# Expert products with a straight read and a PSUM write in four rounds

## The reference

```python
def chunk(args):
    hc, ec, gc = args                       # tokens, chosen experts, their gates
    u = peer_u[ec]
    a = jax.nn.gelu(jnp.einsum("ckd,cd->ck", u, hc).astype(jnp.float32)) * gc
    vv = peer_v[ec]
    return jnp.einsum("ck,ckd->cd", a.astype(vv.dtype), vv)
```

## Time and profile before

| | |
|---|---|
| median of 3 runs | 1580.08 us (1580.06 to 1580.09) |
| the profiled execution, its own time | 1579.2 us |
| its span in the trace | 1577.1 us |
| TensorE clock granted, mean | 0.999 |
| instructions | 33476 |
| scores, about | 325 to 697.6 us |
| values, about | 697.6 to 1062.9 us |

### The profile page before, as it was taken

How to read it: one execution, slowest core, us unless ns; L and a number is a source line. 1 busy time by engine, 2 the same in 40 slices (tenths; PEclk the granted TensorE clock), 3 DMA queues, 4 the chain that set the end, 5 groups by cost and what they waited for, 6 DMA issues and landing times.

```text
span 1577.1 us, 33476 instructions
## 1 busy us (share of the span) xinstructions
PE 1563.8 (99%) x12568; PEld 1472.5 (93%) x12568; DVE 1069.8 (68%) x1867; ACT 881.2 (56%) x1251; POOL 883.7 (56%) x413
## 2 busy tenths in 40 slices
PE   9999999999999999999999999999999999999998
PEld 8999899999999999998888888889999999999998
DVE  7998743879933777778888666676937484455522
ACT  6567766454454444444444445557677654676653
POOL 8786468978886000000000244458875689888886
PEclk9999999999999999999999999999999999999999
DMA  6564335555555555555555655566543356665563
GB/s 222 173 197 154 107 122 192 194 178 195 188 187 189 171 177 171 178 166 175 179 178 163 219 190 190 195 195 188 178 140 111 118 165 190 195 197 190 188 196 124
DMA packets 86217, 277.03 MB, mean 176 GB/s; under 512 B 11232, under 2 KB 18160, under 8 KB 86128
## 3 DMA queue, kind: packets, MB, share of 16 engines
q1 hardware_dynamic: 85712, 274.76, 54.0%
q0 software_dynamic: 272, 1.05, 0.2%
q10 hardware_dynamic: 144, 0.00, 0.0%
HBM read 274.73 MB, written 1.05 MB: 175 GB/s over the span
## 4 chain that ended last, share of the span: by engine, by line
PE 92%; issue 2%; DVE 2%; POOL 2%; ACT 2%; DMA 0%; SPq 0%; DVEq 0%; ACTq 0%; POOLq 0%
PE gemm L683 35%; PE gemm L986 22%; PE gemm L688 18%; PE aux L1272 4%; PE gemm L817 3%; PE aux L966 2%; POOL w_lo L466 1%; PE gemm L704 1%; PE gemm L729 1%; ACT w_hi L1368 1%; PE gemm L1272 1%; PE aux L936 0%; PE gemm L803 0%; PE gemm L710 0%; PE gemm L746 0%
## 5 line engine op out<-in xcount | busy, mean ns | idle before, releaser
L466 POOL TENSOR_TENSOR w_lo<-raw,w_hi 128x1024 fp32r<-128x1024 f32 (+1 forms) x330 | 789.4, 2401 | 282.9 <-ACT w_hi L1368 279.1
L1368 ACT ACTIVATE w_hi<-raw 128x1024 fp32r<-128x1024 f32 (+1 forms) x492 | 514.9, 1048 | 560.5 <-PE gemm L683 310.2
L683 PE MATMUL gemm<-h_hi,w_hi 128*128 128x256 f32 x2096 | 289.2, 280 | 1.1 <-ACT w_hi L1368 1.0
L683 PE MATMUL gemm<-h_lo,w_hi 128*128 128x256 f32 x2144 | 289.9, 277 | 0.0
L688 PE MATMUL gemm<-h_hi,w_lo 128*128 128x256 f32 x2096 | 284.6, 278 | 2.4 <-POOL w_lo L466 1.5
L683 PEld LDWEIGHTS gemm<-h_lo,w_hi 128*128 128x128 f32 x2144 | 266.0, 188 | 0.3 <-issue 0.2
L683 PEld LDWEIGHTS gemm<-h_hi,w_hi 128*128 128x128 f32 x2096 | 261.3, 188 | 4.2 <-issue 1.6
L466 DVE TENSOR_TENSOR w_lo<-raw,w_hi 128x1024 fp32r<-128x1024 f32 x162 | 195.7, 1223 | 102.0 <-ACT w_hi L1368 101.7
L688 PEld LDWEIGHTS gemm<-h_hi,w_lo 128*128 128x128 f32 x2096 | 259.8, 188 | 4.8 <-POOL w_lo L466 3.4
L986 PE MATMUL gemm<-w_hi,act_parts 128*128 128x512 f32 x1008 | 251.0, 391 | 0.4 <-ACT act_parts L1569 0.4
L986 PEld LDWEIGHTS gemm<-w_hi,act_parts 128*128 128x128 f32 x1008 | 188.2, 188 | 38.8 <-issue 0.5
(11 more groups left out here) (436 smaller groups left out, 2044.4 us busy)
## 6 DMA issues: line engine op xcount, KB each, us to landing
raw<-in_w_u SPq DMA_DIRECT2D x128, 512.0 KB, 3.5
raw<-in_w_ev SPq DMA_DIRECT2D x128, 512.0 KB, 3.6
raw<-in_w_up SPq DMA_DIRECT2D x48, 512.0 KB, 3.6
raw<-in_w_gate SPq DMA_DIRECT2D x24, 512.0 KB, 3.7
raw<-in_w_down SPq DMA_DIRECT2D x24, 512.0 KB, 3.5
raw<-in_w_conv_in SPq DMA_DIRECT2D x16, 512.0 KB, 4.4
raw<-in_w_peer_q SPq DMA_DIRECT2D x16, 512.0 KB, 4.0
raw<-in_w_branch SPq DMA_DIRECT2D x24, 288.0 KB, 2.8
```

The source lines that it names most:

```text
L466: eng.tensor_tensor(w_lo[v][:, 0:n], raw[c.raw][v][:, 0:n], w_hi[v][:, 0:n], ALU.subtract).then_inc(lo_ready[v], 1)
L683: mm = pe.matmul(spread(out), w[:, k, :], spread(act_part[:, k, :]), start=(n == k == 0), stop=False)
L1368: act.activation(w_hi[v][:, 0:n], raw[c.raw][v][:, 0:n], ACT.Copy).then_inc(hi_ready[v], 1)
```

## The change

In both expert stages the moving operand is read straight, while PSUM is written in four rounds. A column thus lands in another place of the bank: the columns read as g*64 + j*4 + c (256 of them) are written to j*16 + g*4 + c. `by_groups` names the straight order in the same four indices; gelu, which becomes two activations a chunk, one for each tile's 256 columns, and the four final copies read PSUM in four rounds and write straight, so everything behind them finds the columns as before. All other products keep `spread` on both sides.

```diff
+        def by_groups(tile):
+            return tile.rearrange("p (g j c) -> p g j c", g=4, c=4)
+        def whole(tile):
+            return tile
...
-                        mm = pe.matmul(spread(out), w[:, k, :], spread(act_part[:, k, :]), start=(n == k == 0), stop=False)
+                        mm = pe.matmul(psum_order(out), w[:, k, :], moving_order(act_part[:, k, :]), start=(n == k == 0), stop=False)
...
-                    mm = pe.matmul(spread(out), w[:, k, :], spread(x[0][:, k, :]), start=False, stop=(k == steps - 1))
+                    mm = pe.matmul(psum_order(out), w[:, k, :], moving_order(x[0][:, k, :]), start=False, stop=(k == steps - 1))
...
-                        product(c, P, it)
+                        product(c, P, it, moving_order=whole, psum_order=spread)
...
-                                mm = pe.matmul(gemm[2 * half + tt][:, :], a[:, c.raw, v, tt * P:(tt + 1) * P],
-                                               w[v][:, half * (D // 2):(half + 1) * (D // 2)],
+                                mm = pe.matmul(spread(gemm[2 * half + tt][:, :]), a[:, c.raw, v, tt * P:(tt + 1) * P],
+                                               whole(w[v][:, half * (D // 2):(half + 1) * (D // 2)]),
...
-                act.activation(act_peer[:, plane, :], pair(gemm[c.bank]),
-                               ACT.Gelu_apprx_tanh).then_inc(evacuated[c.bank], 1)
+                for v in range(2):
+                    ins = act.activation(by_groups(plane[v]), spread(pair(gemm[c.bank])[:, v, :]),
+                                         ACT.Gelu_apprx_tanh)
+                ins.then_inc(evacuated[c.bank], 1)
...
-                act.activation(experts[:, 1, half * (D // 2):(half + 1) * (D // 2)], gemm[2 * half + 1][:, :],
+                act.activation(by_groups(experts[:, 1, half * (D // 2):(half + 1) * (D // 2)]),
+                               spread(gemm[2 * half + 1][:, :]),
...
-                dve.tensor_copy(experts[:, 0, half * (D // 2):(half + 1) * (D // 2)],
-                                gemm[2 * half][:, :]).then_inc(experts_moved[0], 1)
+                dve.tensor_copy(by_groups(experts[:, 0, half * (D // 2):(half + 1) * (D // 2)]),
+                                spread(gemm[2 * half][:, :])).then_inc(experts_moved[0], 1)
```

More of the change, by code:

```diff
@@ L657, in _, with product @@
         def _(pe):
-            def product(c, m, it=None, x=(h_hi, h_lo), steps=KD):
+            def product(c, m, it=None, x=(h_hi, h_lo), steps=KD, moving_order=spread, psum_order=spread):
                 for v in range(2):
-                    product_tile(c, v, m, it, x, steps)
+                    product_tile(c, v, m, it, x, steps, moving_order=moving_order, psum_order=psum_order)
             def bank_free(c, it=None):
@@ L667, in bank_free, with product_tile @@
                     pe.wait_ge(evacuated[c.bank], c.bank_use - 1)
-            def product_tile(c, v, m, it=None, x=(h_hi, h_lo), steps=KD, rest=None, between=None):
+            def product_tile(c, v, m, it=None, x=(h_hi, h_lo), steps=KD, rest=None, between=None,
+                             moving_order=spread, psum_order=spread):
                 if v == 0:
@@ L974, in _ @@
                         gate_planes(0, s + 1, it)
-                    product(plan["u"][HALF + s], P, it)
+                    product(plan["u"][HALF + s], P, it, moving_order=whole, psum_order=spread)
             def expert_values(c, it, opens=False):
@@ L1013, in one @@
                     def one(w, a, half, tt, ends=False):
-                        return pe.matmul(gemm[2 * half + tt][:, :], a[:, c.raw, v, tt * P:(tt + 1) * P],
-                                         w[v][:, half * (D // 2):(half + 1) * (D // 2)], start=False, stop=ends,
+                        return pe.matmul(spread(gemm[2 * half + tt][:, :]), a[:, c.raw, v, tt * P:(tt + 1) * P],
+                                         whole(w[v][:, half * (D // 2):(half + 1) * (D // 2)]), start=False, stop=ends,
                                          skip_group_check=True)
@@ L1563, in gelus @@
                         round_weights(order[c.index + 1], it)
-                        gelu(c, bass.ds(it * 2 * BANKS + 2 * s, 2), it)
+                        gelu(c, [act_peer[:, bass.ds(it * 2 * BANKS + 2 * s + v, 1), :].rearrange("p o t -> p (o t)") for v in range(2)], it)
             def round_acts(c, plane, it=0):
```

## The result

The changed kernel takes 1586.09 us (median of 6 runs, 1585.48 to 1588.53) against 1580.26 for the kernel before beside it: ratio 1.0038, 95% interval 1.0028 to 1.0048. It is slower by about 6 us, clear of the 0.2% that this measurement tells from no change. The profiled execution took 1586.07 us with a span of 1584.0, 6.9 more than before.

A forecast was written before the change was run, and what follows sets the result against it. The prediction took TensorE's distance between matmuls as the bound. Scores 0, values -5.8, gelu 0 and copies 0 us gave 1573.4 us against the profiled execution, 1574.3 as a median, range 1560 to 1586.

The forecast's parts named there:

- held by the pair: Scores: stationary load of about 104 ns beside each 107 ns stream sets the matmul distance, so the read's order changes nothing.
- Scores, predicted 0: Expert scores, 3072 matmuls: a straight read with the write kept in four rounds costs 0, bounds -19.4 to +5.8 us.
- the read's order was what helped: Slower rival: scores lose their remedy, +1.9 ns x 3072 = +5.8 us, values gain nothing, 1586; chance 0.15.
- second floor: Scores: loading the stationary operand, about 104 ns, is nearly as long as a 256-column stream and limits the distance too.
- covered twice over: Values: the load (PEld busy 149 of 180 us) is hidden, so the stream alone sets the distance.
- estimate of 104 ns: Load of 128 stationary columns, estimated from rows of 188 ns for 128 columns and 97 for 16.
- Values, predicted -5.8 us: Expert values, 1536 matmuls: writing in four rounds saves 3.8 ns each, -5.8 us, bounds -14.9 to +4.5 us.
- The mixture frees both sides: Rival: same-order read and write hinder each other; scores gain 4.6 to 9.2 us, values 9 to 15, 1561; chance 0.14.
- four rounds cost at 512 columns: Slower rival: the values' write in four rounds takes 229.6 ns a matmul, +4.5 us, 1584.6; chance 0.09.
- Order is worth nothing: Rival: both orders run at the same rate per column in scores and values, -4.3 to +1.5 us, about 1579; chance 0.30.
- Gelu, predicted free: Two gelu activations a chunk add 0.16 us, covered by ScalarE's waiting; cost 0, bounds 0 to 0.5 us.
- The final copies, predicted free: Four final copies with a strided PSUM read: cost 0, under 0.5 us once even at twice the price.

The follow-up runs named there:

- e2: Kernel before with scores read in rounds of 4 and written straight, gelu in two parts, values as before: 1579.49 us, ratio 0.9999.
- e1: Kernel before with scores read and written straight, values as before: 1585.24 us, ratio 1.0032.
- e15: Kernel before with the change's scores part alone (read straight, write in rounds of 4, gelu in two parts): 1586.9 us, ratio 1.0039.
- e10: Kernel before with scores read in eight rounds and written straight, values read straight and written in eight rounds: 1614.77 us.
- e5: Kernel before with scores read and written straight and using only the first 64 stationary columns: 1590.23 us.
- e3: Kernel before with only the values' write in rounds of 4, final copies putting the columns back: 1579.81 us, ratio 1.0000.
- e4: Kernel before with values read and written in rounds of 4, scores and final copies unchanged: 1576.97 us, ratio 0.9980.
- e12: Kernel before with h_hi and h_lo moved by 32 bytes, scores read straight and written in rounds of 4: 1592.39 us.
- e9: e4 with one extra bf16 matmul ahead of the last 480 of the stretch of 528 values matmuls: 1578.03 us, ratio 0.9985.
- e6: Kernel before with scores using only the first 64 stationary columns, read and write in rounds of 4: 1577.51 us.
- e14: The same kernel as e4 measured once more, against the kernel before: 1577.61 us, ratio 0.9980.
- e13: Kernel before with h_hi and h_lo moved by 32 bytes, all orders as before: 1586.84 us.

## Why the prediction was wrong

The bound was read rightly: TensorE paces the kernel and the distance between matmuls is the only thing that moved its time. The failed step is the choice between the sides: the write was taken for the side on which four rounds help, and the load for a cover of the read. In the prediction's words, "If the write is the side on which four rounds help, the stall per 512 columns falls", taken at -5.8 us, and "I expect the distance to be held by the pair and not by the read's order. I take 0" for the scores. The runs show the reverse of both.

- **Scores, predicted 0, measured +5.7 us.** This is the rival "the read's order was what helped", priced at +1.9 ns and 1586 us. e2, e1, e15 and e10 show it: with a read in rounds of 4 the scores run at 114.8 whatever the write does; with a straight read they run at 116.7 or 117.8. That the price came out to the tenth is partly luck. It was half of the stall of a 512-column stream less the stall of a 256-column one, from modelled ends. The distances gave the opposite order at the time: 6.7 ns above the bare stream per 256 columns for the straight values, 8.1 for the scores in rounds. The excess does not scale with the columns, since straight reads show 10.0 to 11.1 ns at 256 and 13.4 at 512, and e1 has stretches that pay 3.0 and not 1.9. What talked me out of this rival was the load of the stationary operand as a second floor. The change refutes that cover by itself: with the loads as they were, the distance rose by 1.9 ns. e5 shows it again: with a load of 133 ns the straight stream was no faster. A load row that is busy without a break was no evidence of a bound, and the 148.65 of 180 us in the values is no evidence of a load "covered twice over"; that came from the estimate of 104 ns.
- **Values, predicted -5.8 us, measured 0.** The write's order has no effect at 512 columns (e3) and none at eight rounds (e10). The size of 3.8 ns was worked out for the right remedy on the wrong side: with the read in rounds (e4), the last 264 matmuls gain 3.4 ns, those beside the gates 1.9 (10.90 us in the mean where 48 took 10.99), the 528 nothing, so the kernel gains 0.2% and not 0.4%.
- **"The mixture frees both sides" and "four rounds cost at 512 columns"** are refuted: the first would have shown in e2 or in the change, the second in e3.
- **"Order is worth nothing"** rested on 113.4 against 114.8 ns per 256 columns. Comparing streams of 256 and of 512 columns hid the order's effect: straight reads give 113.4 per 256 columns in a stream of 512, and 116.7 to 117.8 in a stream of 256.
- **Gelu, predicted free, was free**: 0.66 us for both where 0.76 was allowed, with 1.16 us of idle time behind them, and e2, with two gelus a chunk, takes the time of before. **The final copies, predicted free, were free**: 0.69 and 0.60 us as before, and e3, which has them, takes the time of before.

On the write the Trainium skill ("PSUM - Partial Sum Buffer", Specifications) says that any non-contiguous pattern slows matmuls significantly. No run here shows that for runs of 16 bytes: 226.7 ns straight, in four rounds (e3) and in eight (e10). On the read, the Trainium skill ("Advanced Engine Details and Errata", Memory Cachelines) counts 16-byte lines and asks for two hits on a line for full speed. Every read order here makes four hits on each line, and the distances still lie between 113.3 and 127.0 ns; that rule does not tell these orders apart.

What stays open is the mechanism below the read's order: why, of the orders tried, 64 bytes with pieces of 16 is best, and what selects among several distances of one stream. As the cause of the straight read's cost, the load is excluded by the change and e5, and the write by e1, e2, e3 and e10. Zero data or an idle rest of the core were not tried.

## What to carry to other kernels

Where matmuls follow each other without a gap, the order in which the moving operand is read is worth trying by itself, in both directions: rounds of 4 fp32 columns out of 16 gained 1.6 to 2.5% of the distance at 256 columns (1.4% with the moving tile 32 bytes further) and up to 1.5% at 512, while eight rounds cost 5 to 9% against a straight read. The order of the PSUM write was free in these shapes, in four and in eight rounds of 16 bytes, so use it to put columns in their places: the same order on both sides needs no repair in the evacuation. Compare distances only between streams of the same width, and before you let a second bound cover a cost, test the bound.

## What the runs showed of the hardware

- The distance between fp32r matmuls of one unchanged stream takes one of a few means, holds it for tens of microseconds, and can leave it at a pause: 117.8 then 116.7 ns for straight reads (e1), 117.8, 113.3, 117.8 with the tile moved by 32 bytes (e12), 223.3 or 226.6 for values in rounds (e4, e9). The granted clock was at the upper level throughout.
- The best seen for fp32r at 256 columns was 113.3 ns (e6, and three tiles of e12), 6.6 above the 106.7 of a stream at 2.4 GHz; the best at 512 was 223.3 (e4, e14), 10 above 213.3.
- With the moving tiles 32 bytes further, a read in rounds of 4 went from 114.8 to a mean of 116.1 ns (e13, one execution).
- Eight rounds in the PSUM write cost nothing (226.7), eight rounds in the read 9 to 10 ns at 256 columns in the long stretch and 20 at 512, against straight.
- Halving the stationary columns shortened the load from 188 to 133 ns and made the straight stream slower, 117.8 to 119.0 ns, and the one in rounds faster, 114.8 to 113.3, in the first half of the scores (e5, e6, one execution each).
- PSUM read in four rounds by ScalarE and VectorE costs what a straight read costs: 381 ns for 256 columns against 379 for another ScalarE instruction of that shape, and 0.60 and 0.69 us for 512.
